# Delta rule: the 16-token blocks' powers and inverse kept packed as 32 columns, with VectorE alone taking each power out of its bank

## The reference, cut to what matters

```python
m = jnp.where(strict, jnp.einsum('bhnid,bhnjd->bhnij', kb, k) * decay, 0.0)
t_inv = lax.linalg.triangular_solve(eye + m, jnp.broadcast_to(eye, m.shape),
                                    left_side=True, lower=True, unit_diagonal=True)
u = jnp.einsum('bhnij,bhnjd->bhnid', t_inv, v * beta[..., None])
w = jnp.einsum('bhnij,bhnjd->bhnid', t_inv, kb * jnp.exp(gc)[..., None])
```

## Time and profile before

| | |
|---|---|
| time, median of 3 executions | 3187.47 us (3186.65 to 3192.27) |
| span of the profiled execution | 3188.2 us, 0.7 above the median; no other time is given for it |
| TensorE busy over the span | 3099.4 us (97%) |
| VectorE, ScalarE, GpSimd busy | 2246.8, 1742.8, 821.5 us |
| TensorE's granted clock | 0.99 in the mean, 1.00 in the heads |
| phase of the heads | about 86 to 890 us |

### The profile page before, as it was taken

One profiled execution on the slowest core, in us unless ns is written; L12 is line 12 of the kernel. 1 busy time (PEld: TensorE's weight loads), 2 busy tenths in 40 slices (PEclk: granted clock), 3 DMA queues, 4 the chain that ended last, 5 costly groups with the idle time before them and its releaser, 6 DMA issues.

```text
span 3188.2 us, 63691 instructions
## 1 busy us (share of the span) xinstructions
PE 3099.4 (97%) x19926; PEld 2737.0 (86%) x19926; DVE 2246.8 (70%) x4157; ACT 1742.8 (55%) x3855; POOL 821.5 (26%) x1372
## 2 busy tenths in 40 slices
PE   5999999999999999999999999999999999999998
PEld 4999999999978888888888887888888888888887
DVE  5767777777755788667887767886677654776566
ACT  5565666566644555445555556764555544555444
POOL 1000000000010499888888810770000000000000
PEclk8999999999999999999999999999999999999999
DMA  6454444444467777877777766785666677667764
GB/s 166 115 135 123 125 122 132 128 125 122 132 170 190 195 204 208 226 203 203 202 206 208 211 183 166 231 247 153 185 182 186 189 185 185 183 185 185 185 159 142
DMA packets 1036179, 556.43 MB, mean 175 GB/s; under 512 B 38193, under 2 KB 1023953, under 8 KB 1035585
## 3 DMA queue, kind: packets, MB, share of 16 engines
q1 hardware_dynamic: 969088, 491.18, 57.8%
q10 hardware_dynamic: 58160, 37.63, 4.0%
q0 software_dynamic: 8848, 26.59, 2.7%
HBM read 528.30 MB, written 27.03 MB: 174 GB/s over the span
## 4 chain that ended last, share of the span: by engine, by line
PE 73%; DVE 11%; ACT 7%; issue 6%; DMA 1%; ACTq 1%; DVEq 0%; POOL 0%; SPq 0%; POOLq 0%
PE bank L302 39%; PE bank L303 21%; DVE w_lo L286 5%; ACT w_hi L280 3%; PE bank L633 2%; PE bank L299 1%; ACT T L941 1%; PE bank L300 1%; DVE tiles L1935 1%; ACT L941 1%; DVE normed L1947 1%; DVE tiles L328 1%; PE bank L798 1%; ACT dec L941 1%; DVE y L1775 1%
## 5 line engine op out<-in xcount | busy, mean ns | idle before, releaser
L286 DVE TENSOR_TENSOR w_lo<-raw,w_hi 128x512 fp32r<-128x512 f32 x1856 | 1298.1, 752 | 145.2 <-ACT w_hi L280 137.3
L302 PE MATMUL bank<-act,w_hi 128*128 128x512 f32 x3376 | 1227.5, 405 | 17.5 <-DVE w_lo L286 7.8
L303 PE MATMUL bank<-act,w_lo 128*128 128x256 f32 x4352 | 1224.3, 281 | 0.0
L302 PE MATMUL bank<-mid,w_hi 128*128 128x512 f32 x3072 | 1088.1, 399 | 4.1 <-DVE w_lo L286 3.1
L280 ACT ACTIVATE w_hi<-raw 128x512 fp32r<-128x512 f32 x1856 | 1040.9, 620 | 68.7 <-PE bank L303 44.1
L303 PE MATMUL bank<-mid,w_lo 128*128 128x256 f32 x3072 | 860.7, 280 | 0.0
L303 PEld LDWEIGHTS bank<-act,w_lo 128*128 128x128 f32 x4352 | 827.9, 190 | 0.8
L302 PEld LDWEIGHTS bank<-act,w_hi 128*128 128x128 f32 x3376 | 638.1, 189 | 171.9 <-DVE w_lo L286 11.2
L302 PEld LDWEIGHTS bank<-mid,w_hi 128*128 128x128 f32 x3072 | 579.1, 188 | 147.0 <-issue 3.4
L303 PEld LDWEIGHTS bank<-mid,w_lo 128*128 128x128 f32 x3072 | 581.6, 189 | 0.2 <-issue 0.2
L318 ACT ACTIVATE tiles<-bank 128x256 f32<-128x256 f32 x323 | 123.5, 382 | 541.8 <-PE bank L303 535.6
(11 more groups left out here) (331 smaller groups left out, 3122.6 us busy)
## 6 DMA issues: line engine op xcount, KB each, us to landing
raw<-in_mlp_w_up_dram SPq DMA_DIRECT2D x128, 1024.0 KB, 6.6
raw<-in_mlp_w_down_dram SPq DMA_DIRECT2D x128, 1024.0 KB, 6.2
raw<-in_gdn_w_in_dram SPq DMA_DIRECT2D x96, 1024.0 KB, 6.0
raw<-in_gdn_w_out_dram SPq DMA_DIRECT2D x32, 1024.0 KB, 6.8
raw<-in_ple_w_gate_dram SPq DMA_DIRECT2D x32, 1024.0 KB, 6.3
raw<-in_s_w_out_dram SPq DMA_DIRECT2D x28, 1024.0 KB, 6.8
raw<-in_s_w_in_dram ACTq DMA_DIRECT2D x10, 1024.0 KB, 7.1
c_scratch<-c_pow ACTq DMA_DIRECT2D x32, 256.0 KB, 4.6
```

Source lines behind the costliest of these rows:

```text
L286: eng.tensor_tensor(w_lo[par][:, c], raw[slot][:, c], w_hi[par][:, c].bitcast(F32), ALU.subtract).then_inc(S("lo_ready"), 1)
L302: eng.matmul(a[:, :], w_hi[par][:, w], rhs[:, k0 + kt, :], start=(k0 + kt == 0), stop=False)
L303: mm = eng.matmul(a[:, 0:NT], w_lo[par][:, w], rhs[:, k0 + kt, 0:NT], start=False, stop=(k0 + kt == kend - 1))
```

## The change

The powers of P and the inverse under construction are kept packed. Since only the four diagonal blocks of 32 x 32 of each problem are nonzero, a new tile `pr` [128, 4, 2, 32] holds, for each problem, 32 columns of the transposed power (index 0) and 32 columns of the inverse (index 1). A product takes the full 128 x 128 power as weights (`Pm`, or one of two new tiles `px` that GpSimd clears once) and 32 or 64 packed columns as the moving side, so one `four` gives the next power and the product with the inverse together. There are four of them in a head (32, 64, 64, 32 columns for each problem) in place of six of 128 columns.

ScalarE's three copies of a power are gone. VectorE's `spread` waits for the product, copies the packed power from the bank to `pr`, and transposes it from the bank into the diagonal blocks of `px`, one instruction for each 32 partitions. The transpose of Pm and the last addition, which writes RT, are four instructions each as well. The off-diagonal blocks of RT that must be zero are cleared by GpSimd once for a head, behind the key products. ScalarE's wait for `mid_lo` moves from slot 0 to slot 4. The opening gets a clearing of part of WT and three small additions for `ident32` on VectorE.

```diff
+        pr = gs("pr", [P, 4, 2, 32])
+        px = [gs(f"px{i}", [P, 4, P]) for i in range(2)]
+        ident32 = gs("ident32", [P, 32])
+        block_32 = lambda t_, j: t_[32 * j:32 * j + 32, :, 32 * j:32 * j + 32]
+        pair_of = lambda bk, i: bk[:, 0:256].rearrange("p (m i q) -> p m i q", m=4, i=2)[:, :, i, :]
...
-            def four(bk, lhs, rhs, name, turn_=False):
+            def four(bk, power, first, count, name):
                 for m in range(4):
-                    if turn_:
-                        mm = pe.transpose(bk[:, m * P:(m + 1) * P], lhs[:, m, :], ident)
-                    else:
-                        mm = pe.matmul(bk[:, m * P:(m + 1) * P], lhs[:, m, :], rhs[:, m, :], start=True, stop=True)
+                    mm = pe.matmul(bk[:, m * 64:m * 64 + 32 * count], power[:, m, :],
+                                   pr[:, m, first:first + count, :].rearrange("p i q -> p (i q)"), start=True, stop=True)
                 mm.then_inc(S(name), 1)
...
-                    four(C, PT, Pm, "power_done")
+                    four(C, Pm, 0, 1, "power_done")
                 elif s == 1:
-                    w("power_out", 3, 1)
                     w("RT_ready", 7, 1)
-                    four(A, P2, RT, "R_done")
-                    w("transposed_out", 2, 1)
-                    four(C, P2T, P2, "power_done")
+                    w("power_out", 2, 1)
+                    w("spread_out", 3, 1)
+                    four(A, px[0], 0, 2, "power_done")
                 elif s == 2:
-                    w("power_out", 3, 2)
                     w("RT_ready", 7, 2)
-                    four(A, P4, RT, "R_done")
-                    w("transposed_out", 2, 2)
-                    four(C, P4T, P4, "power_done")
+                    w("power_out", 2, 2)
+                    w("spread_out", 3, 2)
+                    four(C, px[1], 0, 2, "power_done")
...
                 elif s == 3:
-                    w("power_out", 3, 3)
                     w("RT_ready", 7, 3)
-                    four(A, P8, RT, "R_done")
+                    w("spread_out", 3, 3)
+                    four(A, px[0], 1, 1, "R_done")
...
-                if s == 0:
-                    w("mid_lo")
-                    w("power_done", 3, 1)
-                    A_(fl(P2), C[:, :]).then_inc(S("power_out"), 1)
-                elif s == 1:
-                    w("power_done", 3, 2)
-                    A_(fl(P4), C[:, :]).then_inc(S("power_out"), 1)
-                elif s == 2:
-                    w("power_done", 3, 3)
-                    A_(fl(P8), C[:, :]).then_inc(S("power_out"), 1)
-                elif s == 3:
+                if s == 3:
...
                 elif s == 4:
+                    w("mid_lo")
                     w("X_done", 3, 1)
...
+            with gp.Fori(1, KH) as r:
+                gp.wait_ge(S("kk_done"), r + 1)
+                gp.sem_inc(S("RT_read"), 1)
+                gp.memset(RT[0:32, :, 32:64], 0.0).then_inc(S("RT_cleared"), 1)
+                gp.memset(RT[64:96, :, 96:128], 0.0).then_inc(S("RT_cleared"), 1)
+                gp.memset(RT[0:64, :, 64:128], 0.0).then_inc(S("RT_cleared"), 1)
...
-                ve.transpose(fl(PT), fl(Pm)).then_inc(S("PT_ready"), 1)
+                for j in range(4):
+                    last = ve.transpose(pr[32 * j:32 * j + 32, :, 0, :], block_32(Pm, j))
+                last.then_inc(S("PT_ready"), 1)
                 ve.wait_ge(S("PT_ready"), r + 1)
-                TT(RT[:, :, :], PT[:, :, :], ident.unsqueeze(1).to_broadcast([P, 4, P]), ALU.add).then_inc(S("RT_ready"), 1)
-
+                TT(pr[:, :, 1, :], pr[:, :, 0, :], ident32[:, :].unsqueeze(1).to_broadcast([P, 4, 32]),
+                   ALU.add).then_inc(S("RT_ready"), 1)
...
-                def add_to_R(i):
-                    w("R_done", 6, i)
+                def spread(i, bk):
+                    w("power_done", 3, i)
+                    if i < 3:
+                        w("RT_ready", 7, 1)
+                        ve.tensor_copy(pr[:, :, 0, :], pair_of(bk, 0)).then_inc(S("power_out"), 1)
+                    for j in range(4):
+                        last = ve.transpose(block_32(px[(i + 1) % 2], j), pair_of(bk, 0)[32 * j:32 * j + 32])
+                    last.then_inc(S("spread_out"), 1)
+
+                def add_to_R(i, bk):
                     w("RT_ready", 7, i)
-                    TT(fl(RT), A[:, :], fl(RT), ALU.add).then_inc(S("RT_ready"), 1)
+                    TT(pr[:, :, 1, :], pair_of(bk, 1), pr[:, :, 1, :], ALU.add).then_inc(S("RT_ready"), 1)
 
                 low(0)
-                w("power_out", 3, 1)
-                ve.transpose(fl(P2T), fl(P2)).then_inc(S("transposed_out"), 1)
+                spread(1, C)
                 low(1)
-                add_to_R(1)
+                spread(2, A)
+                add_to_R(1, A)
                 low(2)
-                w("power_out", 3, 2)
-                ve.transpose(fl(P4T), fl(P4)).then_inc(S("transposed_out"), 1)
+                spread(3, C)
+                add_to_R(2, C)
                 conv(r, n + 2, 2)
-                add_to_R(2)
...
-                add_to_R(3)
+                w("R_done", 4, 1)
+                w("RT_ready", 7, 3)
+                w("RT_cleared", 3, 1)
+                for j in range(4):
+                    whole = TT(block_32(RT, j), pair_of(A, 0)[32 * j:32 * j + 32], pr[32 * j:32 * j + 32, :, 1, :], ALU.add)
+                whole.then_inc(S("RT_ready"), 1)
```

More of the change, by code:

```diff
@@ L165, in trunk @@
         packed = lambda t_, m: t_[:, :, :].rearrange("p m q -> p (m q)")[:, 64 * m:64 * m + 64]
[L167 to L170, removed]
+        WT, osq, oy = (T[0],) * 3
+        rn, Pm, Dm = (T[1],) * 3
+        sq = T[2]
+        VN, orn = (T[3],) * 2
         g2 = ExitStack()
@@ L1101, in core @@
                 elif s == 5:
-                    w("R_done", 6, 4)
+                    w("R_done", 4, 2)
                     for j in range(4):
@@ L1109, in core @@
                 elif s == 7:
-                    w("R_done", 6, 5)
+                    w("R_done", 4, 3)
                     for j in range(2):
@@ L1121, in core @@
                 elif s == 9:
-                    w("R_done", 6, 6)
+                    w("R_done", 4, 4)
                     A_(RT[0:64, :, 64:128], C[0:64, 0:256].rearrange("p (m q) -> p m q", m=4), scale=-1.0).then_inc(S("RT_ready"), 1)
@@ L1427, in _ @@
                 gp.dma_start(dst, src, allow_slow_non_contiguous=dst.shape[-1] == 1).then_inc(S("side_in"), 16)
+            for t_ in px:
+                gp.memset(t_[:, :, :].rearrange("p m q -> p (m q)"), 0.0).then_inc(S("px_cleared"), 1)
+            gp.memset(RT[:, :, :].rearrange("p m q -> p (m q)"), 0.0).then_inc(S("RT_cleared"), 1)
             gp.wait_ge(S("gc_turned_out"), 1)
@@ L1751, in _ @@
             link(ve.memset(pre[:, :, 0:4], 0.0))
+            link(ve.memset(WT[96:128, :, :].rearrange("p m q -> p (m q)"), 0.0))
             link(TS(onorm[:, :], onorm[:, :], 0.5 * 128 ** -0.5, None, ALU.mult))
@@ L1808, in key_matrix @@
                 ve.wait_ge(S("P_ready"), r + 1)
-                ve.transpose(fl(PT), fl(Pm)).then_inc(S("PT_ready"), 1)
+                for j in range(4):
+                    last = ve.transpose(pr[32 * j:32 * j + 32, :, 0, :], block_32(Pm, j))
+                last.then_inc(S("PT_ready"), 1)
                 ve.wait_ge(S("PT_ready"), r + 1)
-                TT(RT[:, :, :], PT[:, :, :], ident.unsqueeze(1).to_broadcast([P, 4, P]), ALU.add).then_inc(S("RT_ready"), 1)
+                TT(pr[:, :, 1, :], pr[:, :, 0, :], ident32[:, :].unsqueeze(1).to_broadcast([P, 4, 32]),
+                   ALU.add).then_inc(S("RT_ready"), 1)
+            link(TT(ident32[:, :], ident[:, 0:32], ident[:, 32:64], ALU.add))
+            link(TT(ident32[:, :], ident32[:, :], ident[:, 64:96], ALU.add))
+            link(TT(ident32[:, :], ident32[:, :], ident[:, 96:128], ALU.add))
+            ve.wait_ge(S("px_cleared"), 2)
             scalars(0)
```

## The result

| | before | after |
|---|---|---|
| time, median of 4 runs on the same chip | 3187.99 us (3186.65 to 3192.27) | 3246.96 us (3239.68 to 3260.53) |
| ratio, 95% interval | | 1.0194 (1.0164 to 1.0223) |
| span of the profiled run | 3188.2 us | 3238.0 us (its time 3239.68) |
| first load behind the heads (GpSimd's `chunk_no`) | 899.52 us | 965.09 us |
| from there to the end | 2288.7 us | 2272.9 us |

The kernel is 1.9% slower. By the ratio the time is 3249 where before is 3187.5. The forecast was 3230, its range ended at 3248, and the main case's own range at 3240. So sign and place came out as forecast, and the size was too small. The profiled run after is the fastest of the four, so its span understates the loss: 49.8 us, against 59 for the medians.

The account below looks back on a forecast made before the run. VectorE's stretch up to slot 4's product X, with 0.48 us of room, was taken to bound a head. 16 heads x 2.66 = 42.6 us on the 3188.2 span gave 3230.8, median 3230 us, range 3196 to 3248.

Parts of the forecast that it names:

- the main case: Heads: four small VectorE instructions count as four whole durations; 16 x 2.66 = 42.6 us longer, range 3219 to 3240, chance 0.52.
- sign and place: Slower, chance 0.84, through VectorE's longer stretch from slot 21 to slot 4's product X in each head.
- The ring: A head's period runs from X through TensorE to slot 14, ScalarE, then VectorE to next X; the change rewrites VectorE's piece.
- the 0.48 at X: Slot 4: VectorE's RT is ready only 0.48 us, signal included, before TensorE comes to product X.
- TensorE as the pace: Rival, heads: TensorE's 2.06 us less work a head counts, 16 x 2.06 = 33 us gained, 3155; chance 0.10.
- Overlap of small instructions: Rival, VectorE in the heads: each small instruction hides 0.08, X 1.22 later, 20 us lost, 3207; chance 0.22.
- the walk: Slot-by-slot timing of one head, slots 0 to 4: RT 3.14 us later, less 0.48 room, makes a head 2.66 longer.
- The estimate of 0.82 for a product: TensorE: each new `four`, weights 128 wide, takes 0.82 us with 32 or 64 columns; bounds 0.62 and 0.89.
- The clock: TensorE in the heads: the forecast had no term for a lower clock and predicted nothing new in slots 5 to 21.
- I let these two cancel: Opening's four more chained VectorE operations, up to 1.2 us, against a first head that may lose less than 2.66.
- Dearer: Rival: bank reads or GpSimd's clearings hold VectorE up to 1 us more a head, 16 more, 3246; chance 0.10.
- ScalarE: Heads: its three power copies go, but it wasn't last in these slots, and its chain in slots 14 to 21 is unchanged.

Follow-up runs that it names:

- the eighth experiment: Changed kernel with VectorE's order rewritten, no work removed: last splits later, first spread and last additions earlier, query-key product and mask behind RT; 3195.13 us, period 51.80.
- the first experiment: Changed kernel with VectorE's query-key product, one quarter of w_lo and the mask moved behind RT's last additions and transpose Dm; 3222.2 us, period 54.43.
- the third: Changed kernel with the four transposes of each power all reading and writing partitions 0 to 31 (wrong powers); 3236.6 us, period 53.75 at full clock.
- five: Kernel before the change with three unread VectorE multiplications, 1.7 us, added ahead of the second addition to RT; 3188.41 us, period 52.77.
- seven: Kernel before the change without the products P2 x RT and P4 x RT (wrong inverse, VectorE's work the same); 3164.7 us, period 51.17.

## Why the prediction was right about the place and short in the size

- **The ring.** Shown. Padding inside it costs 1.00 of 1.7 and outside it nothing, and the profile after has the forecast's waits in the forecast's places. The room that the padding met, 0.7, is another than the 0.48 at X: it stands in front of slot 3's product. The 0.48 is confirmed by the change itself, where RT is ready 3.89 later (21.37 behind unit q and k, against 17.48) and X comes 3.42 later.
- **TensorE as the pace.** Fell: with its products left out and nothing else in their place, a third of the time came back, and in the change none.
- **Overlap of small instructions.** Fell: four transposes take 1.25 to 1.29, four additions 1.18. Their common start, not their size, is what would have made them overlap.
- **The main case's sum.** This is the step that failed: 16 x 2.66 = 42.6, where the heads became 65.6 longer. About 13 of the missing 23 are the walk and 9 the clock (next point). The period grew by 3.48 and X's delay by 3.42, where the sum had 2.66. The missing 0.76 is spread over the walk: about 0.35 in four sets of transposes with the copies and additions around them (1.25 to 1.29 where 1.20 stood, and the gap behind each), 0.18 in the products of slots 1 and 2 (1.14 from the product's start to VectorE's next instruction in both, where 1.06 and 1.04 stood), 0.18 in the signal ahead of slot 2's product (0.23 from 428.75 to 428.98, where it was 0.05), and the rest in steps under 0.05. The estimate of 0.82 for a product was met once, without a wait in front (0.81 in the eighth experiment); behind a wait it's 0.91 and 0.94, and X, the same product as before, keeps TensorE for 0.80 (436.71 to 437.51) where it was 0.72. That the wait makes the difference isn't shown, since slot 3's product takes 0.91 too (431.86 to 432.77) with no wait in its row. These are the mis-sized terms, 0.82 in the period: 16 x 0.82 = 13 us.
- **The clock.** The sum put this at nothing. It's 6.3 in four turns, most of the 3.0 in the first period and a part of the last head, and 9.3 by filling the waits. The earlier trace rows showed a clock of 1.00, and I carried it over to a kernel whose waits I had just worked out, nearly 5 us in each head. "I let these two cancel" for the first head was wrong too: its period grew by 6.45 rather than by less than 2.66.
- **Dearer.** Its 3246 is 1 us from the median, and that is luck: neither of its two causes is there. A transpose takes 302 ns from SBUF and 312 from the bank (medians below), so bank reads cost 0.12 us a head. The Trainium skill's 62 cycles for a bank's reader ("VectorE: DVE Perf Modes", the section on the trn2 errata) would be 0.065 each. The trace shows 0.010. GpSimd's clearings take 0.19, 0.20 and 0.31 and nothing waits for them.

```profile
L1813 DVE STREAM_TRANSPOSE pr<-T x64: 299/302/308, 84.4 to 923.3; 32x128 f32<-32x128 f32 x64
```

```profile
L1851 DVE STREAM_TRANSPOSE px<-bank x192: 293/312/324, 87.2 to 932.9; 32x128 f32<-32x128 f32 x192
```

- **ScalarE.** Its three copies are gone, 64.8 us less work in the same 804, and none of it was on the path. It waits instead, 12.3 us in a head, for VectorE's convolution.

```profile
ACT tiles L943 <- DVE y L1778: 86.0, 7, 12.3
```

## What to carry to other kernels

An engine at 74% can be the one that sets the pace: before giving it work, read who waits for it and by how much it's ahead in that slot, and count a chain of small instructions by whole durations when each starts at other partitions. When the walk says that TensorE will wait, allow about 0.1 more for the small product behind each wait, and don't carry over a full clock: here it fell in some heads. If a rewrite shortens TensorE and lengthens another engine's chain, the order of that engine's work has to be rewritten with it: here order alone (VectorE's, and the place of one tanh on ScalarE) took the loss from 1.9% to nothing that can be told, and the change itself gained nothing even then.

## What the runs showed of the hardware that I hadn't expected

**A clock that falls in a busy stretch.** In the kernel after the stretches at 1.2 GHz lie behind X, where TensorE is always busy, 1.5 to 1.7 us after its last wait ended, and only in every third head, though all the heads have the same waits. In the first experiment they come in every fourth head and begin in slot 1, 0.8 us behind the wait there; in the third, in about every second head, 0.1 to 0.9 us behind the wait for X. The Trainium skill ("TensorE: Matmul & The Clock Gate", Part 1) has two rates and lets recent activity choose, which agrees with the two levels seen. Why one head in two, three or four is hit isn't shown by any run here.

**Two paces of the same products.** Behind the heads the products of 512 and 256 columns come either every 0.353 or every 0.346 us, with the granted clock at 1.00 in both. The product of 512 columns in 2400 to 2900 us, durations in ns, before and then after:

```profile
L302 PE MATMUL bank<-act,w_hi x859: 395/398/404, 2399.9 to 2884.0; 128*128 128x512 f32 x172
```

```profile
L308 PE MATMUL bank<-act,w_hi x916: 390/392/586, 2403.4 to 2899.7; 128*128 128x512 f32 x184
```

A chunk takes 5.65 us at one pace and 5.55 at the other, over 50 chunks near the end. The pace holds for long stretches. At the end of the program the slower one is found in before and in seven of the ten experiments, the faster in after and in three experiments (one, five, seven). The code behind the heads is the same in all of them, so the pace doesn't follow from it. It explains most of the 15.8 us that this run of after has back (13.5 of them arise over the last 150 chunks), and may be what scatters the single runs. What chooses it stays open. Against effects of 10 us a period read in the trace told more than the time of one run.
